# Requesting every second weight slab of the experts from ScalarE instead of SyncE

## The chip, the cores and the metric

The kernel runs on one core of a Trainium2 chip. The metric is the device time of one execution in microseconds (us). A core has five engines that run side by side, each with an instruction stream of its own: TensorE (PE), VectorE (DVE), ScalarE (ACT), GpSimd (POOL) and SyncE (SP), which here only issues DMA transfers. Transfers issued by SP run in the DMA queue that the profile calls q1, those issued by ACT in q10, and POOL's in q0. All the queues are served by the same 16 DMA engines.

## The reference

Two blocks of layers work on 256 tokens of width 1024. The first block has a short convolution, a SwiGLU layer, latent attention, and a mixture of eight experts. The second has four SwiGLU layers, block attention and a state-space mixer. The change touches the mixture alone:

```python
probs = jax.nn.softmax((ht @ router).astype(jnp.float32), axis=-1)
vals, idx = lax.top_k(probs, TOP_K)                      # TOP_K = 2
gates = ...                                              # the two weights of a token, zeros elsewhere
for e in range(N_EXPERTS):                               # 8
    out = out + gates[:, e:e + 1] * swiglu(ht, w_gate[e], w_up[e], w_down[e])   # hidden width 2048
```

## The kernel before

**Slabs.** All large weights are packed in the order of their use into 436 slabs of up to 128 x 2048 fp32 (1 MB). A slab is loaded from HBM into one of six slots of the SBUF tile `raw`. Then it is split in two, so that fp32 products can be built from fp32r products: ACT copies it, rounded, to `whi` (`split_hi`, L704 to L710), and DVE subtracts to get the rest, `wlo` (`split_lo`, L1298 to L1304). `whi` and `wlo` have three slots each. TensorE then makes three products per tile: high by high, high by low, low by high (`three`).

**Semaphores.** `raw_full[slot]` rises when a slab has landed. `slab_hi` counts ACT's copies, `slab_split` DVE's subtractions, and `slab_used` the slabs that TensorE is done with. ACT's copy of slab m waits until the slab has landed and until TensorE has used slab m - 3. The load of slab s waits for `slab_split >= s + 1`: the slab six places before has been split, so its slot is free.

**Queues.** SP issues all the slab loads, one after another, each as soon as its slot is free (`load`, L521 to L524). ACT issues few transfers, POOL a few small ones.

**The expert stage.** It has 8 experts with 24 slabs each, so 192 slabs, here called m = 0 to 191 (`ffn_stage` with `gates`). An expert's hidden width is cut in 8 chunks. Each chunk needs two slabs of gate and up weights and one of down weights. The program takes a step per slab: in step k of an expert, TensorE works on slab k, while ACT and DVE split slab k + 2 (`ahead`). No expert has more than 128 tokens to work on here, so the function `routed` runs: the tokens of an expert are gathered by small products with a 0/1 matrix (`gather` on TensorE, `operand` on ACT and DVE), and one tile of 128 rows goes through the layer. The function `ffn`, for more tokens, does not run in this stage.

**Results.** An expert's result, 128 x 1024, is copied from PSUM by ACT at step k = 2 of the next expert and stored to the DRAM tensor `y_rows`, from ACT's queue (`result`, L818 to L824). After the seventh such store has landed, POOL issues four indirect transfers that gather, for every token, the rows of its experts from `y_rows` back to SBUF (`y_back`, L617 to L623), 128 x 1024 each. DVE adds them to `x` in the last expert, at steps 13, 15, 18 and 20 (`add_back`, L1720 to L1725). The first of these waits until all four gathers have landed, and it stands in DVE's stream right behind the subtraction of slab m = 183. The subtraction of m = 184 comes behind it.

**What sets the order.** The streams of all engines are written out by hand; loops over the experts (`positions`, `each_expert`) repeat a body with register offsets. Nothing is scheduled by a planner.

Of the kernel before, what the change touches and what calls it, by code (L numbers as in the profile page):

```python
# [31 lines left out]
RAW = 6  # L32
SPLIT = 3
SLAB = 2048
EPS = 1e-6
F_EXPERT = 2048
D_FF = 2816
# [23 lines left out]
def program(nc, a, out):  # L61
    ctx = ExitStack()
    with ctx:
        def sb(name, shape, dt=F32):
            return ctx.enter_context(nc.sbuf_tensor(name, shape, dt))
# [4 lines left out]

        raw = sb("raw", [P, RAW, SLAB])
        whi = sb("whi", [P, SPLIT, SLAB], F32R)
        wlo = sb("wlo", [P, SPLIT, SLAB], F32R)
        raw_full = [sem(f"raw_full{n}") for n in range(RAW)]
        slab_hi = sem("slab_hi")
        slab_split = sem("slab_split")
# [442 lines left out]
        @block.sync  # L519
        def _(sp):  # L520
            def load(s, slot, width):  # L521

                sp.wait_ge(slab_split, s + 1)
                sp.dma_start(raw[:, slot, 0:width], slab_of(s, width)).then_inc(raw_full[slot], 16)  # L524

            def slab_of(s, width):
                return a["slabs"][s if isinstance(s, int) else bass.ds(s, 1)].rearrange(
                    "p n -> p n" if isinstance(s, int) else "o p n -> (o p) n")[:, 0:width]

            def ffn_loads(f):  # L530
                def at(k, i, ex):
                    load(f.s0 + k + 6 * i + 3 * f.C * ex, (f.s0 + k) % RAW, SLAB)
                positions(sp, f, at)

            for t in range(NT):
                sp.dma_start(x[:, t, :], a["x"].rearrange("(t p) d -> p t d", p=P)[:, t]).then_inc(x_loaded, 16)
            for f in stages_used:
                if f.kind == "ffn":
                    ffn_loads(f)
                else:  # L540
                    for n, width in enumerate(WIDTHS.get(f.kind, [])):
                        load(f.s0 + n, (f.s0 + n) % RAW, width)
            for n in range(2):
                cs = slice(512 * n, 512 * (n + 1))
                sp.wait_ge(x_ready, x_total - 1 + n)
                sp.dma_start(out.rearrange("(t p) d -> p t d", p=P)[:, :, cs], x[:, :, cs]).then_inc(out_done, 16)
            sp.wait_ge(out_done, 32)
# [155 lines left out]
        def _(act):  # L703
# [8 lines left out]
            def ahead(base, k, i=0, per=0):  # L712
                if base + k + 2 < total_slabs:
                    split_hi(base, k + 2, i, per)

            def squares(f):

                if f.x0 == 0:
                    act.wait_ge(x_loaded, 16 * NT)
                else:  # L720
                    act.wait_ge(x_ready, f.x0)
                for t in range(NT if f.deferred else 1):
                    act.activation(hn[:, t], x[:, t], ACT.Square, accum_out=n_sum[:, f.m, t:t + 1]).then_inc(norm_sum, 1)
# [34 lines left out]
            def ffn(f, opening=False, rest=False):  # L758
                C = f.C

                def t_hi(c, i, ex, to=hT):
                    act.wait_ge(tp_full, f.u0 + c + 1 + 2 * i + C * ex)
                    act.activation(to[0], tp[:, (f.u0 + c) % 2], ACT.Copy).then_inc(tp_hi, 1)  # L763

                def at(k, i, ex):
                    kind, c = ffn_kind(f, k, ex)
                    ahead(f.s0, k, i, C // 2 * ex)
                    if k == 0:
                        norm_late(f.before)
                        norm_squares(f.before)  # L770
                    if k == 1:
                        act.wait_ge(norm_rstd, f.m)
                    if kind == "up_b":
                        act.wait_ge(gu_half, f.c0 + c + 1 + 2 * i + C * ex)
                        act.activation(silu_g[:, 0, :], gu[:, 0, 0:FC], ACT.Silu,
                                       scale=n_rstd[:, f.m - 1, 0:1]).then_inc(gu_silu, 1)
                        used(act, f.s0, k, i, C // 2 * ex)
                        act.activation(silu_g[:, 1, :], gu[:, 1, 0:FC], ACT.Silu,  # L778
                                       scale=n_rstd[:, f.m - 1, 1:2]).then_inc(gu_silu, 1)
                    elif kind == "up_a" and k:  # L780
                        t_hi(c - 1, i, ex)
                    elif ends_with(f, k, ex):
                        t_hi(C - 1, 0, ex, hT_last)
                    elif kind == "down" and k == 3 * C - 1:
                        norm_early(f.after)
                positions(act, f, at, opening, rest)
# [13 lines left out]
            def routed(f):  # L800
                C = f.C
                v, g0 = V_FFN, KT

                def operand(q, kt, odd, base=2):

                    if kt % 4 == 0 and not odd:
                        act.wait_ge(gathered, 2 * q + kt // 4 + 1)
                    o = xg_odd if odd else xg_hi[0]
                    r = act.activation(o[:, kt * P:(kt + 1) * P], acc[in_pair(kt, odd, base)], ACT.Copy, scale=col(v, g0 + kt))
                    if kt % 2 and odd:  # L810
                        r.then_inc(xg_hi_done, 1)

                def odd_operand():

                    act.drain()
                    act.activation(xg_hi[1], xg_odd, ACT.Copy).then_inc(odd_hi_done, 1)

                def result(e, odd):  # L818

                    act.wait_ge(y_stored, 16 * e)  # L820
                    act.activation(y_out[odd], acc[:, 0:2, :].rearrange("p b n -> p (b n)"), ACT.Copy).then_inc(yg_hi_done, 1)
                    act.wait_ge(yg_hi_done, e)
                    act.dma_start(y_rows[(e - 1) * P:e * P] if isinstance(e, int) else y_rows[bass.ds((e - 1) * P, P)],
                                  y_out[odd]).then_inc(y_stored, 16)  # L824

                def last_result(n):

                    if n:
                        used(act, f.s0, 3 * C * EXPERTS - 1)
                    else:  # L830
                        act.wait_ge(y_half, 1)
                    act.activation(yg_hi[:, 512 * n:512 * n + 512], acc[:, n], ACT.Copy).then_inc(yg_hi_done, 1)

                def at(k, ex, first, last, pair):
                    kind, c = ffn_kind(f, k, ex)
                    if last and k == 3 * C - 1:
                        last_result(0)
                        last_result(1)
                    ahead(f.s0, k, 0, C // 2 * ex)
                    if k == 2 and not first:  # L840
                        used(act, f.s0, 1, 0, C // 2 * ex)
                        result(ex, 1 - pair[0])
                    if kind == "up_b":
                        used(act, f.s0, k, 0, C // 2 * ex)
                        act.activation(silu_g[:, 0, :], gu[:, c % 2, 0:FC], ACT.Silu).then_inc(gu_silu, 2)
                    t = 0 if first and k == 2 else c + 1 if kind == "down" and k != 3 * C - 1 else None
                    if t is not None:
                        act.wait_ge(tp_full, f.u0 + t + 1 + C * ex)
                        bank = tp[:, (f.u0 + t) % 2]
                        if t == 1 and last:  # L850
                            act.activation(put, bank[:, 2 * P:4 * P], ACT.Copy)
                        to = hT_spare if last and t == C - 1 else hT
                        act.activation(to[0][:, 0:2 * P], bank[:, 0:2 * P], ACT.Copy).then_inc(tp_hi, 1)
                    odd, q = pair
                    if odd and not last:
                        for n in range(2):
                            if GATHER_AT[n] < k <= GATHER_AT[n] + 4:
                                for j in range(2):
                                    operand(q + 1, 4 * n + k - GATHER_AT[n] - 1, j)
                    if not odd and k == ODD_AT:  # L860
                        odd_operand()

                act.sem_inc(y_stored, 16)
                for kt in range(KT):
                    for j in range(2):
                        operand(0, kt, j, (2, 0)[kt // 4])
                each_expert(act, at)

            def mla(f):
# [2235 lines left out]
```

## Time and profile before

| | |
|---|---|
| device time, median of 3 runs | 2086.67 us (2085.4 to 2086.81) |
| span of the profiled execution | 2084.0 us |
| busy: PE, DVE, ACT, POOL | 98%, 68%, 57%, 5% |
| TensorE clock granted | 1.000 throughout |
| moved by DMA | 467.11 MB, of it 455.24 MB in q1 |
| expert stage, about 425 to 978 us of the span | 339 to 384 GB/s in slices of 52 us; elsewhere 305 at the start, then 122 to 195 GB/s |

The span runs from the first to the last instruction of one profiled execution; it is the only time that the profile gives for it. The 2.7 us between it and the median lie around the span. All times of the trace below count from the start of the span. "Landing" is the time from the start of a DMA issue to the semaphore that tells of its end. An engine's name with a q (ACTq, SPq) marks an instruction of its sequencer, the part that waits and issues, while the engine's own arithmetic may go on. A row names the line of the code, so L1303 is the subtraction that makes `wlo`, L710 the copy that makes `whi`.

### The profile page before, as it was taken

The numbers are of one execution on the slowest core, as the hardware profiler recorded it, in microseconds if no ns is written. First come the engines' busy times: TensorE is split into PE (matmuls) and PEld (weight loads), VectorE is DVE, ScalarE is ACT, GpSimd is POOL, SyncE is SP. The second block draws the span as 40 slices with busy tenths as digits, with TensorE's granted clock in tenths as the row PEclk, the third lists the DMA queues.
The fourth block names the chain that finished last, engine by engine and source line by source line (L and its number), as shares of the span: only waits on it lengthen the run. The fifth ranks groups of instructions, "written<-read, shape, count | busy, mean of one in ns | idle before, by whom it ended". The sixth has DMA issues, their size and how long they took to land.

```text
span 2084.0 us, 27770 instructions
## 1 busy us (share of the span) xinstructions
PE 2046.0 (98%) x10189; PEld 1713.0 (82%) x10189; DVE 1409.6 (68%) x1529; ACT 1198.0 (57%) x1374; POOL 93.9 (5%) x140
## 2 busy tenths in 40 slices
PE   9999999999999999999999999999999999999999
PEld 9988887778878878787788877888888899888887
DVE  6655457698888988889444685445555579785444
ACT  4454458677777777776344565444444465874442
POOL 1010001000000000010100010000000000220000
PEclk9999999999999999999999999999999999999999
DMA  8555434389999999998555443555455455445551
GB/s 305 187 183 185 180 140 145 122 326 362 361 362 370 357 362 351 367 384 339 183 185 194 160 164 145 185 195 184 178 184 181 147 180 194 162 152 182 190 192 41
DMA packets 68267, 467.11 MB, mean 224 GB/s; under 512 B 7776, under 2 KB 8176, under 8 KB 13520
## 3 DMA queue, kind: packets, MB, share of 16 engines
q1 hardware_dynamic: 63616, 455.24, 59.0%
q10 hardware_dynamic: 3536, 8.10, 1.2%
q0 software_dynamic: 1024, 2.56, 0.5%
q8 instruction: 57, 0.93, 0.2%
q14 instruction: 34, 0.28, 0.0%
HBM read 461.11 MB, written 4.75 MB: 224 GB/s over the span
## 4 chain that ended last, share of the span: by engine, by line
PE 84%; DVE 6%; ACT 5%; issue 3%; DVEq 1%; ACTq 0%; POOL 0%; POOLq 0%
PE gu L2146 15%; PE gu L2148 15%; PE gu L2147 15%; PE acc L2146 9%; PE acc L2148 9%; PE acc L2147 9%; DVE wlo L1303 3%; ACT whi L710 2%; PE acc L2242 2%; PE acc L2244 2%; PE acc L2243 2%; PE tp L2256 1%; PE tp L2175 1%; PE acc L2696 1%; PE tp L2728 1%
## 5 line engine op out<-in xcount | busy, mean ns | idle before, releaser
L1303 DVE TENSOR_TENSOR wlo<-raw,whi 128x2048 fp32r<-128x2048 f32 (+2 forms) x435 | 987.1, 2272 | 365.6 <-ACT whi L710 365.2
L710 ACT ACTIVATE whi<-raw 128x2048 fp32r<-128x2048 f32 (+1 forms) x436 | 827.4, 1899 | 214.5 <-PE acc L2148 165.9
L2146 PE MATMUL gu<-whi,actA_hi 128*128 128x512 f32 (+1 forms) x1448 | 575.4, 397 | 3.6 <-DVE actA_lo L1324 1.5
L2147 PE MATMUL gu<-wlo,actA_hi 128*128 128x512 f32 (+1 forms) x1448 | 563.0, 389 | 1.3 <-issue 1.3
L2148 PE MATMUL gu<-whi,actA_lo 128*128 128x512 f32 (+1 forms) x1448 | 564.0, 389 | 0.0
L2146 PEld LDWEIGHTS gu<-whi,actA_hi 128*128 128x128 f32 x1448 | 272.0, 188 | 59.8 <-issue 5.3
L2148 PEld LDWEIGHTS gu<-whi,actA_lo 128*128 128x128 f32 x1448 | 271.7, 188 | 59.1 <-issue 1.5
L2147 PEld LDWEIGHTS gu<-wlo,actA_hi 128*128 128x128 f32 x1448 | 272.4, 188 | 52.0
L2146 PE MATMUL acc<-whi,hT_hi 128*128 128x512 f32 x656 | 256.6, 391 | 4.4 <-DVE wlo L1303 4.1
L2148 PE MATMUL acc<-whi,hT_lo 128*128 128x512 f32 x656 | 255.6, 390 | 0.0
L2147 PE MATMUL acc<-wlo,hT_hi 128*128 128x512 f32 x656 | 255.4, 389 | 0.0
L2146 PEld LDWEIGHTS acc<-whi,hT_hi 128*128 128x128 f32 x656 | 123.1, 188 | 33.4 <-DVE wlo L1303 3.8
L763 ACT ACTIVATE hT_hi<-tp 128x512 fp32r<-128x512 f32 x50 | 29.9, 598 | 202.2 <-PE tp L2256 202.2
L2148 PEld LDWEIGHTS acc<-whi,hT_lo 128*128 128x128 f32 x656 | 123.2, 188 | 25.8
L2147 PEld LDWEIGHTS acc<-wlo,hT_hi 128*128 128x128 f32 x656 | 123.2, 188 | 24.8
L1371 DVE TENSOR_TENSOR hT_lo<-tp,hT_hi 128x512 fp32r<-128x512 f32 x50 | 34.6, 692 | 117.6 <-ACT hT_hi L763 117.6
L2146 PE MATMUL acc<-whi,actA_hi 128*128 128x512 f32 (+1 forms) x240 | 98.0, 409 | 0.0
L778 ACT ACTIVATE silu_g<-gu,n_rstd 128x256 f32<-128x256 f32 x55 | 26.1, 475 | 119.3 <-PE gu L2148 119.3
L2148 PE MATMUL acc<-whi,actA_lo 128*128 128x512 f32 (+1 forms) x240 | 91.7, 382 | 0.0
L2147 PE MATMUL acc<-wlo,actA_hi 128*128 128x512 f32 (+1 forms) x240 | 91.4, 381 | 0.0
L1386 DVE SCALAR_TENSOR_TENSOR h_tok<-gu,n_rstd,silu_g 128x256 f32<-128x256 f32 x110 | 52.9, 481 | 48.0 <-ACT silu_g L778 47.9
L2242 PE MATMUL acc<-actB_hi,whi 128*128 128x256 f32 x256 | 73.2, 286 | 0.5 <-DVE wlo L1303 0.5
(448 smaller groups left out, 2257.2 us busy)
## 6 DMA issues: line engine op xcount, KB each, us to landing
raw<-in_slabs SPq DMA_DIRECT2D x427, 1024.0 KB, 4.9
y_rows<-big ACTq DMA_DIRECT2D x7, 512.0 KB, 7.4
raw<-in_slabs SPq DMA_DIRECT2D x4, 576.0 KB, 3.7
hT_hi<-cum_rows ACTq DMA_DIRECT2D x8, 256.0 KB, 3.1
hT_lo<-cum_rows ACTq DMA_DIRECT2D x8, 256.0 KB, 4.3
raw<-in_slabs SPq DMA_DIRECT2D x2, 768.0 KB, 4.1
raw<-in_slabs SPq DMA_DIRECT2D x2, 640.0 KB, 3.9
x<-in_x SPq DMA_DIRECT2D x2, 512.0 KB, 4.8
```

The costliest lines, as they stand in the source:

```text
L710: act.activation(whi[:, n0 % SPLIT, 0:w], raw[:, n0 % RAW, 0:w], ACT.Copy).then_inc(slab_hi, 1)
L763: act.activation(to[0], tp[:, (f.u0 + c) % 2], ACT.Copy).then_inc(tp_hi, 1)
L778: act.activation(silu_g[:, 1, :], gu[:, 1, 0:FC], ACT.Silu, scale=n_rstd[:, f.m - 1, 1:2]).then_inc(gu_silu, 1)
L1303: dve.tensor_tensor(wlo[:, n0 % SPLIT, 0:w], raw[:, n0 % RAW, 0:w], whi[:, n0 % SPLIT, 0:w].bitcast(F32), ALU.subtract).then_inc(slab_spli ...
L1371: dve.tensor_tensor(to[1], tp[:, (f.u0 + c) % 2], to[0].bitcast(F32), ALU.subtract).then_inc(tp_read, 1)
L1386: dve.scalar_tensor_tensor(h_tok[:, t, :], gu[:, t, FC:2 * FC], n_rstd[:, f.m - 1, t:t + 1], silu_g[:, t, :], ALU.mult, ALU.mult).then_inc ...
L2146: pe.matmul(o, xh, wh, start=start, stop=False)
L2147: pe.matmul(o, xh, wl, start=False, stop=False)
L2148: return pe.matmul(o, xl, wh, start=False, stop=stop)
L2242: pe.matmul(o, w[0][:, kt, bs], aT_hi[:, kt], start=kt == 0, stop=False)
L2243: pe.matmul(o, w[0][:, kt, bs], aT_lo[:, kt], start=False, stop=False)
L2244: r = pe.matmul(o, w[1][:, kt, bs], aT_hi[:, kt], start=False, stop=kt == KT - 1)
```

## The change

SP asks only for some of the slabs of the expert stage: the first nine (m = 0 to 8) and after them those with even m. The odd ones, m = 9, 11, ..., 191, are asked for by ACT in its own queue: at step k (odd), behind the copy of slab k + 2, ACT waits for the same semaphore value and issues the load of slab k + 6. These are 92 loads. Slots, semaphores, splitting and products stay as they are, and so do the loads of all other stages.

```diff
+BESIDE = 6
+FIRST_BESIDE = 3 + BESIDE
...
+            def expert_loads(f):
+                n = 3 * f.C
+                def at(k, ex, first):
+                    if k % 2 == 0 or (first and k < FIRST_BESIDE):
+                        load(f.s0 + k + n * ex, (f.s0 + k) % RAW, SLAB)
+                for k in range(n + 2):
+                    at(k, 0, True)
+                with sp.Fori(1, f.experts - 1) as ex:
+                    for k in range(2, n + 2):
+                        at(k, ex, False)
+                for k in range(2, n):
+                    at(k, f.experts - 1, False)
...
-                if f.kind == "ffn":
+                if f.kind == "ffn" and f.gates is not None:
+                    expert_loads(f)
+                elif f.kind == "ffn":
                     ffn_loads(f)
...
+            def load_beside(f, k, ex):
+                n = 3 * f.C
+                m = k + BESIDE
+                if f.gates is None or m % 2 == 0 or isinstance(ex, int) and n * ex + m >= n * f.experts:
+                    return
+                s = f.s0 + m + n * ex
+                act.wait_ge(slab_split, s + 1)
+                act.dma_start(raw[:, (f.s0 + m) % RAW, :], a["slabs"][s if isinstance(s, int) else bass.ds(s, 1)].rearrange(
+                    "p n -> p n" if isinstance(s, int) else "o p n -> (o p) n")).then_inc(raw_full[(f.s0 + m) % RAW], 16)
...
                     ahead(f.s0, k, 0, C // 2 * ex)
+                    load_beside(f, k, ex)
                     if k == 2 and not first:
                         used(act, f.s0, 1, 0, C // 2 * ex)
                         result(ex, 1 - pair[0])
```

Where ACT's stream changes: the start of an expert in the loop, where the result of the expert before it is stored (`y_rows<-big`). Before, from the store on, with the copies of two slabs:

```order
305 L821 ACTIVATE big<-acc 128x1024 [waits y_stored]
306 L823 ISA [waits yg_hi_done]
307 L823 DMA y_rows<-big 128x1024
308 L708 REGISTER_ALU [waits raw_full2]
309 L710 ACTIVATE whi<-raw 128x2048 [waits slab_used]
310 L449 REGISTER_ALU
311 L845 ACTIVATE silu_g<-gu 128x256 [waits slab_used]
312 L710 ACTIVATE whi<-raw 128x2048 [waits slab_used,raw_full3]
```

The same place of ACT's stream now (the lines have moved: L710 is L729, L823 is L855; the load is L743):

```order
317 L853 ACTIVATE big<-acc 128x1024 [waits y_stored]
318 L855 ISA [waits yg_hi_done]
319 L855 DMA y_rows<-big 128x1024
320 L727 REGISTER_ALU [waits raw_full2]
321 L729 ACTIVATE whi<-raw 128x2048 [waits slab_used]
322 L742 ISA
323 L743 ISA [waits slab_split]
324 L743 DMA raw<-in_slabs 128x2048
325 L451 REGISTER_ALU
326 L878 ACTIVATE silu_g<-gu 128x256 [waits slab_used]
327 L729 ACTIVATE whi<-raw 128x2048 [waits slab_used,raw_full3]
```

A load with its wait and a register instruction now stands between the copy of 128x2048 and the silu behind it. It is in the same queue as the store just ahead of it.

Where SP's stream changes: the end of its loop over the experts and the loads of the last expert behind it. Before (L524 is the load, L461 the loop over the experts, L472 that of the next stage):

```order
102 L523 REGISTER_ALU
103 L524 ISA [waits slab_split]
104 L524 DMA raw<-in_slabs 128x2048
105 L461 REGISTER_ALU
106 L461 COMPARE_AND_BRANCH
107 L524 DMA raw<-in_slabs 128x2048 [waits slab_split] x24
108 L472 UNCONDITIONAL_BRANCH
```

The same place of SP's stream now:

```order
66 L525 REGISTER_ALU
67 L526 ISA [waits slab_split]
68 L526 DMA raw<-in_slabs 128x2048
69 L546 REGISTER_ALU
70 L546 COMPARE_AND_BRANCH
71 L526 DMA raw<-in_slabs 128x2048 [waits slab_split] x13
72 L474 UNCONDITIONAL_BRANCH
```

The 24 loads in a row of before are 22 of the last expert and the first two of the next stage. Of these 13 are left with SP; of the other 11 slabs the loads are ACT's. The streams of PE, DVE and POOL are the same as before.

## Rows read from the trace of the kernel before

**Rows 1.** Windows: length, PE busy, PEld, DVE, ACT, POOL, clock, DMA share, GB/s.

```profile
431.00:925.00 494.00, 487.40 (x2220) 396.62 (x2219) 430.94 (x321) 372.51 (x338) 0.45 (x1) 1.00 0.95 363
925.00:956.00 31.00, 29.93 (x135) 24.05 (x134) 28.76 (x20) 22.11 (x19) 7.64 (x4) 1.00 1.00 411
```

**Rows 2.** Waits of PE in the expert stage, 430 to 970: total, times, longest.

```profile
PE tp L2728 <- DVE h_tok L1739: 4.4, 8, 0.9
PE acc L2146 <- DVE wlo L1303: 3.0, 5, 0.7
```

**Rows 3.** The slab loads, line L524, 431 to 925.

```profile
L524 SPq DMA_DIRECT2D raw<-in_slabs x168: 327/333/343, 431.6 to 924.6; - x168
DMA to landing us min/median/max: 4.7/6.8/9.3
```

**Rows 4.** The first and the last of the four gathers, line L621, with their landings.

```profile
L621 POOL DMA_INDIRECT big<-y_rows,back_row x1: 1187/1187/1187, 924.5 to 924.5; - x1
DMA to landing us min/median/max: 10.0/10.0/10.0
...
L621 POOL DMA_INDIRECT big<-y_rows,back_row x1: 2577/2577/2577, 931.0 to 931.0; - x1
DMA to landing us min/median/max: 14.8/14.8/14.8
```

**Rows 5.** DMA queues, 929 to 943: packets, MB, share of 16 engines.

```profile
q1 hardware_dynamic: 521, 3.82, 65.7%
q0 software_dynamic: 539, 1.97, 35.4%
```

**Rows 6.** Timeline of DVE at the first `add_back` (L1724): start, length.

```profile
944.35 2.29 DVE L1303 TENSOR_TENSOR wlo<-raw,whi 128x2048 fp32r<-128x2048 f32 x1 [0.37 <-ACT whi L710]
946.73 1.29 DVE L1724 SCALAR_TENSOR_TENSOR x<-big,x 128x1024 f32<-128x1024 f32 x1
...
948.27 4.48 DVE L1303 TENSOR_TENSOR wlo<-raw,whi 128x2048 fp32r<-128x2048 f32 x2
```

**Rows 7.** Timeline of PE where slab m = 184 begins.

```profile
950.61 0.50 PE L2146 MATMUL acc<-whi,hT_hi 128*128 128x512 f32 x1 [0.17 <-DVE wlo L1303]
```

**Rows 8.** The seven stores of results, line L823; below, the landing of the last alone.

```profile
L823 ACTq DMA_DIRECT2D y_rows<-big x7: 343/347/374, 487.8 to 914.0; - x7
DMA to landing us min/median/max: 4.6/7.4/10.4
...
DMA to landing us min/median/max: 9.6/9.6/9.6
```

**Rows 9.** Timeline of ACT in the state-space stage: a DMA issue without a wait.

```profile
1785.37 0.63 ACT L1142 ACTIVATE aux<-aux 128x512 f32<-128x512 f32 x1
1785.37 0.33 ACTq L1125 DMA_DIRECT2D hT_hi<-cum_rows  x1
1785.90 1.90 ACT L710 ACTIVATE whi<-raw 128x2048 fp32r<-128x2048 f32 x1
```

**Rows 10.** Timeline of ACT behind the last store, which had waited for its copy.

```profile
914.42 1.92 ACT L710 ACTIVATE whi<-raw 128x2048 fp32r<-128x2048 f32 x1 [0.49 <-ACT big L821]
```

**Rows 11.** Waits of ACT in the expert stage, 430 to 970.

```profile
ACT silu_g L845 <- PE gu L2148: 52.7, 54, 3.2
ACT hT_hi L853 <- PE tp L2728: 50.8, 56, 2.7
ACT whi L710 <- PE gu L2148: 25.1, 45, 0.7
```

**Rows 12.** The load of slab m = 185, line L524, with its landing.

```profile
L524 SPq DMA_DIRECT2D raw<-in_slabs x1: 328/328/328, 935.3 to 935.3; - x1
DMA to landing us min/median/max: 11.3/11.3/11.3
```

**Rows 13.** Timeline of ACT: the copies of slabs m = 181 and m = 185.

```profile
936.87 1.91 ACT L710 ACTIVATE whi<-raw 128x2048 fp32r<-128x2048 f32 x1
...
947.81 1.92 ACT L710 ACTIVATE whi<-raw 128x2048 fp32r<-128x2048 f32 x1 [0.62 <-PE gu L2148]
```

More of the change, by code:

```diff
@@ L767, in at @@
                     ahead(f.s0, k, i, C // 2 * ex)
+                    if k >= 2:
+                        load_beside(f, k, ex)
                     if k == 0:
@@ L839, in at @@
                     ahead(f.s0, k, 0, C // 2 * ex)
+                    load_beside(f, k, ex)
                     if k == 2 and not first:
```

## The prediction, made before the changed kernel ran

> **What bounds the kernel now.** I read the busy shares by window first. In the expert stage TensorE is busy 487.40 of 494 us and the clock is granted in full; DVE (430.94) and ACT (372.51) have time left [rows 1]. The DMA engines are busy 95% at 363 GB/s, and 100% at 411 GB/s in the last 31 us [rows 1], so the second question is whether a slab is ever late. The waits say no. TensorE waits 7.4 us in the whole stage, and both rows name DVE [rows 2]. ACT's waits, which would hold a late slab, all name TensorE [rows 11]. A load takes 4.7 to 9.3 us to land until 925 [rows 3]. So the loads have time, though little bandwidth is free. I then looked for the other users of the DMA engines in the stage, because the change touches nothing but queues: ACT's seven stores of results [rows 8] and POOL's four gathers [rows 4], which use the queue q0 beside q1 [rows 5]. Last came what waits for them: DVE's first `add_back` [rows 6], and behind it TensorE [rows 7].
>
> **Part 1: 92 issues come to ACT.** An issue takes about 0.35 us of ACT's sequencer [rows 8]. In the state-space stage such an issue starts in the same instant as an ACTIVATE of 0.63 us, and the next ACTIVATE starts 0.53 us later, at the usual 0.1 us before the end of the one ahead [rows 9]. So an issue that waits for nothing runs beside the arithmetic and costs nothing. Here each new issue stands behind a copy of 1.9 us [rows 13] and waits for `slab_split` at a value that belongs to slab m - 6, which TensorE is about to use or using; in nearly all steps it is there. The other end is the store, which has to wait for its copy: ACT then idles 0.49 us in front of the next copy [rows 10]. At that price 92 issues are 45 us of ACT, but ACT waits 128.6 us in the stage (52.7 + 50.8 + 25.1) [rows 11], 0.67 us a step. Only where it does not wait would the price show: the 7 turns from expert to expert and the 12 odd steps (9, 11, 17 and 19 of experts 1, 3 and 5) in which it also makes the next operands. That is 19 x 0.49 = 9.3 us at most. I take 0, since rows 9 is the same kind of instruction in the same position; the cover is the copy.
>
> **Part 2: the odd slabs are asked for later.** SP asked for slab m as soon as its slot was free; ACT asks when its copy of slab m - 4 has begun. For m = 185 that is 936.87 instead of 935.3, 1.6 us later [rows 12, 13]. SP's request came 12.5 us before the copy of the slab at 947.81 [rows 12, 13]; 10.9 us would be left, and until 925 the slowest landing is 9.3 us [rows 3]. Cost 0 there. At m = 185 the landing took 11.3 us, because the gathers run at that time, and the copy would be 0.4 us late if it stayed so [rows 12, 13]; that is the upper end, and it lies inside the delay of part 4.
>
> **Part 3: SP loses 92 issues.** SP waited for free slots before each, and nothing waits for SP. 0.
>
> **Part 4: a third queue beside the gathers.** This is the term that I find. From 929 to 943 the queues q1 (slabs) and q0 (gathers) both have work all the time. They are served packet for packet, 521 against 539, which gives 3.82 against 1.97 MB in 14 us, 414 GB/s together [rows 5]. The first gather lands at 924.5 + 10.0 = 934.5, the fourth at 931.0 + 14.8 = 945.8 [rows 4]: three intervals of 3.77 us. A gather is 128 x 1024 fp32, 0.524 MB, so 1.27 us of each interval are its own at 414 GB/s and 2.50 us are q1's. Now the slabs come in two queues. If each queue takes its turn, a gather needs 1.27 + 2 x 2.50 = 6.27 us. The fourth then lands three such intervals behind the first, at 934.5 + 18.8 = 953.3. That holds while both slab queues have work. Together they would get 5.00 of 6.27 us of 414 GB/s, 330 GB/s, and the stage wants 363 [rows 1], so their backlog grows and they stay full.
>
> What waits for it: DVE has done the subtraction of m = 183 at 944.35 + 2.29 = 946.64 and starts the first `add_back` at 946.73 [rows 6]. The fourth gather had landed 0.9 us before. Landing at 953.3, it holds DVE for 6.6 us. Behind the `add_back` stand DVE's part of the hidden rows and the subtraction of m = 184 [rows 6]. TensorE already waits 0.17 us for just this subtraction [rows 7], so there is no slack, and the 6.6 us go to the end in full; ACT and SP, which follow TensorE and DVE by semaphores, shift along. The later three `add_back` find their data in place.
>
> The bounds. Upward: the first gather is stretched too, by one more slab's share, 2.5 us, so 9.1 us. Downward: the gathers start when the last store has landed, which took 9.6 us, with other stores at 4.6 [rows 8]. Beside half the slabs in q1 it could land up to 5.0 us sooner, so 1.6 us. The slabs themselves gain from the third turn in this stretch, but ACT does not wait for them [rows 11], so 0. I take 6.6, because the gathers' own spacing is the nearest row.
>
> The Trainium skill (page "DMA: Bandwidth & Descriptors", section "Queues, rings and completion order") says that each DMA engine goes round robin between the queue rows that it has work for, packet by packet. No row here shows three full queues at once; by that rule the third turn is real and the second rival below falls. The rule's packet may hold several descriptors, where the trace's records of q1 and q0 alternate one for one; for the spacing both give the same.
>
> **Sum.** 2084.0 (span) + 0 + 0 + 0 + 6.6 = 2090.6 us; with the 2.7 us that lie around the span before (2086.67 - 2084.0) this is 2093.3 us. I forecast 2093.
>
> **Rivals.**
> First, ACT pays for its issues: they do not hide under the copy. For it: the 0.49 us of rows 10. Against it: rows 9, and ACT's waits. Price 9.3 us: 2096.
>
> Second, on the other side, no change: the gathers keep every second turn, because the DMA engines take the two slab queues in one turn, or one of them is always empty when the other is full. Then the fourth gather lands before 946.7, DVE waits for nothing, and everything else hides under TensorE. For it: all rows show but two queues at a time, and at 363 of 411 GB/s [rows 1] a slab queue may run dry for a while. It decides as soon as the fourth gather is less than 0.9 us later than before. Time: 2086.7. In between, if a store that lands sooner gives most of the delay back, the time is 2088 to 2090.
>
> Third, faster: two queues feed the DMA engines more evenly, slabs land sooner, and some of the 7.4 us of TensorE's waits [rows 2] go. Against it: both rows name DVE, which itself waits for no slab. At most 2086.7 - 7.4 = 2079, more likely 2082.
>
> **How the numbers follow.** The third queue that holds up the gathers: 0.60, at 2093, its own range 2088 to 2096. No change: 0.27, at 2086.7. ACT pays: 0.08, at 2096. Faster: 0.05. What a measurement of this kernel can tell from no change is 0.2%, 4.2 us, so 2082.5 to 2090.9 is "same". Of the first case about 0.10 falls below 2090.9. Slower: 0.50 + 0.08 = 0.58; same: 0.27 + 0.10, less a little at the edge, 0.37; faster: 0.05. The range from 2085.5 to 2097 holds the no-change case, the forecast and its upper end, and leaves out the faster case and a little above.
>
> **What would show it.** In the profile after: q10 with some 96 MB more and q1 with as much less. The gathers of L621 about 6.3 us apart in their landing instead of 3.8, the last at 953 or so. In DVE's rows a wait of 6 to 7 us in front of the first `add_back`, put down to POOL's DMA, and one of the same length of TensorE for `wlo` behind it. ACT's waits for TensorE otherwise about as before, ACT's DMA issues starting within 0.5 us of the start of a copy, and no wait of ACT for a slab. The expert stage up to 925 as long as before, to 1 us. Part 4 is wrong if the gathers keep their spacing, or if the last store lands so early that they are done by 946.7. Part 1 is wrong if ACT's copies start later behind TensorE than before. The forecast as a whole is wrong if the stretch from 925 to 978 is no longer than now.

## The result, and the profile after

| | before | changed |
|---|---|---|
| median of 9 runs | 2085.87 us (2085.34 to 2087.02) | 2091.1 us (2089.43 to 2093.45) |
| ratio to before, 95% interval | | 1.0026, 1.0017 to 1.0035 |
| span of the profiled execution | 2084.0 us | 2091.7 us |

The change costs 5.2 us. The forecast was 2093.3 us, a loss of 6.6 us, all of it from a third full DMA queue beside the gathers. The profiled execution of the changed kernel is the slowest of its nine (2093.45 us), so what the profile shows is more than the 5.2 us of the medians. The line numbers have moved: L524 is L526, L710 is L729, L1303 is L1336, L1724 is L1757, L621 is L640, L823 is L855. ACT's loads of slabs are L743.

First, is the loss spread over the stage? Up to 925 us it is not. The window of 494 us before the gathers, with columns as in [rows 1]:

```profile
431.00:925.00 494.00, 487.72 (x2222) 396.85 (x2221) 431.22 (x321) 372.44 (x338) 4.63 (x2) 1.00 0.95 362
```

TensorE is as busy as before (487.72 against 487.40 us), at full clock. The copies of the slabs start within 0.7 us of their times before, up to m = 183. ACT's own issues hide. Two of them on ACT's timeline:

```profile
572.15 1.91 ACT L729 ACTIVATE whi<-raw 128x2048 fp32r<-128x2048 f32 x1
572.25 0.34 ACTq L743 DMA_DIRECT2D raw<-in_slabs  x1
```

The issue begins 0.1 us after the copy and is over long before it. ACT waits for TensorE as much as before, 50.8, 55.4 and 24.3 us where [rows 11] has 52.7, 50.8 and 25.1; the 4.6 us more in the second are the stall below.

What the two queues do change, all along the stage, is how long a slab takes to land. The slab loads of ACT and then of SP, up to 925, where [rows 3] has a median of 6.8 and a maximum of 9.3:

```profile
DMA to landing us min/median/max: 4.7/7.9/10.7
...
DMA to landing us min/median/max: 4.8/8.0/10.3
```

TensorE never waits for it there, but the margin is thin. From the landing of a slab to its copy there were at least 3.7 us before (m = 8 to 175); now it is 0.2 us at m = 81. Not all of the longer landing need be the change's: two other kernels with SP alone (e3b, e7) have a median of 5.6 to 5.7 us there, where this profile of before has 6.8. Behind 925 us the margin is gone. Slab m = 185 landed 11.6 us after its request, and its copy had to wait:

```profile
948.40 1.92 ACT L729 ACTIVATE whi<-raw 128x2048 fp32r<-128x2048 f32 x1 [1.11 <-DMA raw<-in_slabs]
```

The copy began 0.6 us later than before [rows 13]. It cost nothing here, because DVE, which needs it next, was held up for longer by the gathers.

Now the gathers. The first and the last of the four, as in [rows 4]:

```profile
L640 POOL DMA_INDIRECT big<-y_rows,back_row x1: 2297/2297/2297, 920.1 to 920.1; - x1
DMA to landing us min/median/max: 11.8/11.8/11.8
...
L640 POOL DMA_INDIRECT big<-y_rows,back_row x1: 2687/2687/2687, 928.1 to 928.1; - x1
DMA to landing us min/median/max: 23.1/23.1/23.1
```

They land at 931.9 and 951.2: three intervals of 6.4 us, where before there were 3.77. And they start 4.4 us sooner, since the last store, which took 9.6 us [rows 8], now takes this:

```profile
DMA to landing us min/median/max: 5.1/5.1/5.1
```

The last store lands sooner in every kernel in which ACT asks for slabs at that place (3.0 to 5.7 us) than in those in which SP asks for all the slabs there (7.7 to 9.6 us).

The queues from 929 to 943, where [rows 5] has two, with packets, MB and share:

```profile
q10 hardware_dynamic: 332, 2.45, 41.7%
q1 hardware_dynamic: 304, 2.20, 37.9%
q0 software_dynamic: 340, 1.26, 22.1%
```

The three queues get 332, 304 and 340 packets: equal turns. The gathers' 1.97 MB of before have become 1.26 MB. DVE at the first `add_back`, where [rows 6] shows no wait:

```profile
951.30 1.28 DVE L1757 SCALAR_TENSOR_TENSOR x<-big,x 128x1024 f32<-128x1024 f32 x1 [4.57 <-DMA big<-y_rows,back_row]
```

And TensorE at slab m = 184, where [rows 7] has a wait of 0.17 us:

```profile
955.17 0.79 PE L2179 MATMUL acc<-whi,hT_hi 128*128 128x512 f32 x1 [4.64 <-DVE wlo L1336]
955.76 0.63 PE L2180 MATMUL acc<-wlo,hT_hi 128*128 128x512 f32 x1
```

The reader should look at the lengths too: 0.63 us for a product that takes 0.39 elsewhere. The windows show why, in the column behind POOL, the granted clock:

```profile
956.00:960.00 4.00, 4.00 (x10) 3.07 (x10) 3.91 (x4) 0.00 (x0) 0.00 (x0) 0.50 0.77 256
...
987.00:992.00 5.00, 4.29 (x12) 3.43 (x13) 3.54 (x5) 2.18 (x3) 0.00 (x0) 0.66 0.16 25
```

TensorE stands still from 950.5. The granted clock falls to 0.50 at 953.8, still within the wait, and is back at 960.6; 0.50 is the lower of its two levels (1.2 instead of 2.4 GHz). It falls once more from 987.9 to 991.3, where the stage ends and TensorE has waited 1.5 us as it does before (1.49 us there too); in the profile of before, the clock stayed at 1.00 there.

By the starts of the copies against those of before, the shift is 0.1 us at m = 183, 6.0 us at m = 187, and 7.7 us from four slabs into the next stage to the end. So of the 7.7 us of this execution, 4.6 are the wait, 1.4 the low clock behind it, and 1.7 the second fall of the clock. This second fall is not peculiar to the changed kernel. The profile of e6 below, a kernel without any stall of DVE or TensorE at the gathers, has the same fall at the same place, and the copies slip by 1.6 us there:

```profile
979.00:984.00 5.00, 4.36 (x12) 3.44 (x13) 3.47 (x5) 2.12 (x2) 0.00 (x0) 0.66 0.10 15
```

The nine runs fall into two groups: in five the mean clock is 0.999, with 2089.4 to 2091.1 us, in four 0.997, with 2091.5 to 2093.5. A stretch of 6.8 us at half clock takes 0.0016 off the mean and the low clock at the end of the span up to 0.0003 more, so a run with only the first fall of the profile would show 0.998, as e11 does. In the five runs, the median one among them, the clock was thus low for a shorter time. Where, no profile shows; runs of the kernel before have a mean of 0.999 too, from 2085.4 us up.

### The profile page after: what moved, and what is told of

It reads as the page before. It is cut to its first block, busy times and chain, and to the rows that moved or that the text cites. A ratio compares the mean times of both kernels' runs of the same rounds, so it can differ in the third digit from the quotient of the medians.

```text
span 2091.7 us, 27698 instructions
## 1 busy us (share of the span) xinstructions
PE 2049.5 (98%) x10189; PEld 1715.4 (82%) x10189; DVE 1409.3 (67%) x1529; ACT 1197.5 (57%) x1374; POOL 95.5 (5%) x140
## 4 chain that ended last, share of the span: by engine, by line
PE 82%; DVE 6%; ACT 5%; issue 3%; DMA 2%; DVEq 1%; ACTq 1%; POOL 0%; SPq 0%; POOLq 0%
PE gu L2179 15%; PE gu L2181 15%; PE gu L2180 15%; PE acc L2179 9%; PE acc L2181 9%; PE acc L2180 9%; DVE wlo L1336 3%; ACT whi L729 2%; PE acc L2275 2%; PE acc L2277 2%; PE acc L2276 2%; PE tp L2289 1%; DMA big<-y_rows,back_row 1%; PE tp L2208 1%; PE acc L2729 1%
## 5 line engine op out<-in xcount | busy, mean ns | idle before, releaser
L1336 DVE TENSOR_TENSOR wlo<-raw,whi 128x2048 fp32r<-128x2048 f32 (+2 forms) x435 | 986.9, 2271 | 367.9 <-ACT whi L729 367.3
L729 ACT ACTIVATE whi<-raw 128x2048 fp32r<-128x2048 f32 (+1 forms) x436 | 827.3, 1899 | 216.0 <-PE acc L2181 161.9
```

Source lines behind the costliest of these rows:

```text
L729: act.activation(whi[:, n0 % SPLIT, 0:w], raw[:, n0 % RAW, 0:w], ACT.Copy).then_inc(slab_hi, 1)
L1336: dve.tensor_tensor(wlo[:, n0 % SPLIT, 0:w], raw[:, n0 % RAW, 0:w], whi[:, n0 % SPLIT, 0:w].bitcast(F32), ALU.subtract).then_inc(slab_spli ...
```

## The experiments

The theory is that of the prediction: the third full queue beside the four gathers. The rivals: ACT pays for its issues, and slabs come late all along the stage. Each time below is a median, beside runs of the kernel before on the same chip (2085.6 to 2085.9 us). The intervals of the ratios reach about 0.0009, or 1.9 us, to either side, so smaller differences are not told apart from nothing. Where the text prices a smaller one, it goes by the traces.

**e1: the last expert's loads by SP alone.**

```diff
-                if f.gates is None or m % 2 == 0 or isinstance(ex, int) and n * ex + m >= n * f.experts:
+                if f.gates is None or m % 2 == 0 or isinstance(ex, int) and ex == f.experts - 1:
```

SP's loads of the last expert take every k from 9 on.

> The changed kernel, but in the last expert SP asks for the odd slabs too (m = 177 to 191), so ACT issues 84 loads instead of 92, and none while the gathers run. Theory (a third busy queue beside the four gathers delays the first add_back): the gathers land 3.8 us apart again, DVE does not wait for them, and the time is that of before, 2086 us, within 1.5 us. Rival (ACT pays for each issue): 84 of 92 issues are left, so 84/92 of the 5.2 us stay, 2090.6 us. Rival (two queues make slabs late throughout the stage): also about 2090.5 us.

Measured: 2085.54 us, ratio 0.9999 (0.9990 to 1.0008). The first and the last gather:

```profile
L641 POOL DMA_INDIRECT big<-y_rows,back_row x1: 2405/2405/2405, 922.9 to 922.9; - x1
DMA to landing us min/median/max: 10.0/10.0/10.0
...
L641 POOL DMA_INDIRECT big<-y_rows,back_row x1: 2579/2579/2579, 930.7 to 930.7; - x1
DMA to landing us min/median/max: 13.5/13.5/13.5
```

They land at 932.9 and 944.3, 3.8 us apart, and DVE does not wait. The 84 loads that ACT still issues cost nothing that these runs can tell. Slabs land just in time here too: the copies wait 1.8 us for them, four times in all, at no visible cost. So both rivals fall as the cause of the 5.2 us, and without eight loads of the last expert there is no loss. Whether these eight alone make the whole of it is asked next.

**e2 and e10: only the last expert's odd slabs by ACT.** The other half, run twice.

```diff
-                    if k % 2 == 0 or (first and k < FIRST_BESIDE):
+                    if k % 2 == 0 or not (isinstance(ex, int) and ex == f.experts - 1) or k < FIRST_BESIDE:
...
-                if f.gates is None or m % 2 == 0 or isinstance(ex, int) and n * ex + m >= n * f.experts:
+                if f.gates is None or m % 2 == 0 or not (isinstance(ex, int) and ex == f.experts - 1) or m >= n:
```

> The other half: SP asks for all slabs of the experts 0 to 7, except for the odd ones m = 177 to 191, which ACT asks for. Only 8 issues come to ACT. Theory: the whole loss is here; the last gather lands at 950 to 953, DVE waits 4 to 7 us, time 2090 to 2092 us. Rival (ACT pays per issue): 8/92 of 5.2 us, 2086.4 us. Rival (late slabs all along the stage): at most 1 us of loss, 2087 us.

> e2_last_expert_by_act once more, for a second profile. Its 11 times lay between 2085.3 and 2093.7 us; in its profile the last store took 3.0 us to land and the last gather landed at 947.3, 0.7 us too late. Theory: the time follows the landing of the last gather. A profile in which it lands at T shows DVE's wait T - 946.7, and the time is about 2086 us plus this wait, plus 1 to 3 us where TensorE's clock falls.

Measured: 2087.26 us, ratio 1.0009 (1.0000 to 1.0018), with single runs from 2085.3 to 2093.7; the second run (e10, a single time) took 2087.96 us. This was not the 2090 to 2092 us that I expected: the eight loads are needed for the loss (e1), but alone they make only some 1.4 us. The mechanism is there: the gathers land 6.1 and 6.3 us apart. But the store took 3.0 us, so they began at 917.8, and the last one landed at 947.3 in the first profile and 948.7 in the second. DVE's wait in the first:

```profile
DVE x L1757 <- DMA big<-y_rows,back_row: 0.9, 1, 0.9
```

The second run does not fit the rule written for it: DVE was late itself by then and waited 0.2 us only, while the copies of slabs had slipped by up to 2.4 us one after another from m = 179 on, because slabs landed late: ACT waited 5.5 us for them in four waits, for m = 179, 181, 183 and 185, all its own. The price came in another way, 2.0 us in the end. So late slabs, the rival that e1 put aside, can cost time too, though only in this stretch. What differs from the changed kernel is what lies in the queues when the gathers begin. In e2 a slab took 5.6 us (median) to land up to then, in the changed kernel 8, and there the store (5.1 us) and the first gather (11.8 against 11.0) are slower too. That the 3.8 us between e2 and the changed kernel come from this backlog fits the traces, but it was not isolated.

**e5: all slabs of the last expert by ACT, from m = 176 on.** The condition `m % 2 == 0` goes, and SP's loads of the last expert end at k = 7.

> SP asks for all slabs up to m = 175, ACT for all 16 from m = 176 on. While the gathers run there are again only two full queues, q10 (slabs) and q0, and ACT issues twice as many loads there as in the changed kernel. Theory (number of full queues): the gathers land 3.8 us apart, DVE waits at most 1 us, 2086 to 2087 us. Rival (what counts is that ACT issues loads in this stretch): worse than with the odd ones alone, 2092 us or more.

Measured: 2086.45 us, ratio 1.0003 (0.9994 to 1.0012). The gathers land at 927.1 and 938.8, 3.9 us apart, and DVE does not wait. Twice the loads from ACT in the very stretch, but two full queues instead of three: for the spacing of the gathers the number of queues decides, not who issues.

**e3 and e3b: the adds later.** In the changed kernel and, as control, in the one before.

```diff
-BACK_AT = (13, 15, 18, 20)
+BACK_AT = (16, 18, 20, 22)
```

> The changed kernel with the four add_back at steps 16, 18, 20 and 22 of the last expert instead of 13, 15, 18 and 20. The first then stands where DVE arrives at about 955, behind the last landing at 951. Theory: the gathers still land 6.3 us or more apart, but nobody waits for them; time 2086 to 2088 us, where the 2 us above before are for the adds that now stand closer to the end of the stage. TensorE's clock stays at its full share, since there is no stall. Rival (ACT pays, or the slabs are late): the loss stays, 2091 us.

> The kernel before with the four add_back at steps 16, 18, 20 and 22. Control for e3_late_add_back (2087.3 us): if the 1.4 us that e3 keeps are the price of the late adds, this one takes 2087.3 us too; if they come from the third queue, 2085.9 us.

Measured: e3 2087.31 us, ratio 1.0007 (0.9998 to 1.0016); e3b 2086.03 us, ratio 1.0001 (0.9993 to 1.0010). In e3 the last gather lands at 951.5, as late as in the changed kernel, and the first `add_back` finds it there:

```profile
955.56 1.28 DVE L1757 SCALAR_TENSOR_TENSOR x<-big,x 128x1024 f32<-128x1024 f32 x1
```

The clock of the profiled execution stays at 1.000. So some 3.8 of the 5.2 us are the wait with its clock, taken away with the queues as they are. The late adds cost nothing that e3b can tell. Of the 1.4 us that e3 keeps, its interval holds nothing as well; if they are real, they are not the price of the late adds, as I had written, but may be late slabs. In its trace the copies wait 2.3 us, four times, for slabs that have not landed (`ACT whi L729 <- DMA raw<-in_slabs: 2.3, 4, 1.7`).

**e7: the stall alone.** The kernel before, with `BACK_AT = (11, 15, 18, 20)`.

> The kernel before with the first add_back at step 11 instead of 13. DVE gets there at 941.1 and the last gather lands at 945.8, so it makes DVE wait 4.7 us with no change of the queues. It prices the stall alone. If a stall costs its length, 2085.9 + 4.5 = 2090.4 us. If TensorE's clock falls behind it, as it did in the changed kernel (0.50 from 956 to 960), 1.5 to 3 us more: 2092 to 2093 us.

Measured: 2086.19 us, ratio 1.0011 (1.0001 to 1.0021), and the median says little: eight of the twelve runs lie between 2085.4 and 2088.3 us, four between 2091.1 and 2096.3, these at a mean clock of 0.997 or 0.998. The profiled one is among the eight:

```profile
943.99 1.28 DVE L1724 SCALAR_TENSOR_TENSOR x<-big,x 128x1024 f32<-128x1024 f32 x1 [3.08 <-DMA big<-y_rows,back_row]
```

A wait of 3.1 us gave a span 2.5 us longer, with the clock at 1.00. I had reckoned with a wait of 4.7 us, but here the last store landed sooner. Seven of the eight runs took at most 2086.3 us, no more than before; how long DVE waited in them is not known, so this kernel prices no stall of 4.6 us. It does show that a stall can pass without the clock's falling. Which stall does so is open, and its length alone does not tell: TensorE's wait was 3.3 us here, and in e4 below a wait of 2.4 us was followed by a fall.

**e4 and e6: all slabs by ACT, in its loop and with the loop written out.** In e4 ACT issues 184 loads; in e6 its loop over the experts is unrolled besides.

```diff
-                    if k % 2 == 0 or (first and k < FIRST_BESIDE):
+                    if first and k < FIRST_BESIDE - 1:
...
-                if f.gates is None or m % 2 == 0 or isinstance(ex, int) and n * ex + m >= n * f.experts:
+                if f.gates is None or isinstance(ex, int) and n * ex + m >= n * f.experts:
...
-                each_expert(act, at)          # e6 only
+                for e in range(EXPERTS):
+                    for k in range(2, 3 * (F_EXPERT // FC) + (0 if e == EXPERTS - 1 else 2)):
+                        at(k, e, e == 0, e == EXPERTS - 1, (e % 2, e // 2))
```

> ACT asks for all slabs of the experts from m = 8 on (184 loads), SP for none of them. Twice the issues on ACT, but again one slab queue beside the gathers. Theory: the gathers land 3.8 us apart again and the loss is gone, 2086 us, unless the last store, which now stands behind slabs in its own queue, lands later than the 9.6 us of before: each us of that is a us of wait from 0.9 us on, 2086 to 2089 us. Rival (ACT pays per issue): twice the 5.2 us, 2096 us.

> As e4_all_by_act (ACT asks for all slabs from m = 8 on), but ACT's loop over the experts is written out, with constants in place of registers. e4 lost its 9.6 us in two jumps, 3.2 us and 5.1 us, at the first step of the second and the third pass of ACT's loop, not in equal parts per issue. If the jump back is what costs (the longer loop body has to be brought in again), the loss is gone: 2086 to 2087 us. If it is the issues, it stays: 2095 us.

Measured: e4 2095.5 us, ratio 1.0046 (1.0032 to 1.0059); e6 2084.22 us, ratio 0.9992 (0.9983 to 1.0000). Taken alone e4's time is what the rival "ACT pays per issue" gave. Its trace says otherwise. The gathers are 3.8 us apart, and the time goes in two places, m = 76 and m = 124. These are the first steps of the second and the third pass of ACT's loop:

```profile
630.30 1.92 ACT L729 ACTIVATE whi<-raw 128x2048 fp32r<-128x2048 f32 x1 [2.98 <-PE gu L2181]
...
778.23 1.91 ACT L729 ACTIVATE whi<-raw 128x2048 fp32r<-128x2048 f32 x1 [4.74 <-issue]
```

The slabs had landed 9 us before, so ACT waited for none of them. Nor was it TensorE, which the profile names at the first place: it ran without a gap until 632, 0.3 us behind its times of before, and there the same copy began at 627.2. TensorE waited 2.4 and 4.2 us for the `wlo` behind these copies. After each wait the clock was at 0.50 for 3.4 us, which makes up much of what is left of the 9.6 us over before: the shift is 2.8 us at m = 76 and 0.6 more by m = 80. From there to the second place, some 45 steps with an issue each, it grows by 0.6 us. With the loop written out, both stops are gone, and 184 issues from ACT cost nothing (e6 against e8 below, 2084.22 and 2084.18 us). That the jump brings in the loop body again and finds it late is my reading; shown is only that the stops go with the loop.

**e8, e9 and e11: the written-out loop by itself.** e8 is the kernel before with ACT's loop unrolled as in e6, e9 has DVE's unrolled too, and e11 is the changed kernel with ACT's unrolled.

> The kernel before (SP asks for all slabs) with ACT's loop over the experts written out. e6_all_by_act_unrolled took 2084.2 us, 1.7 less than before. If that gain is the written-out loop (constants in place of register instructions, no jump back), it is here too: 2084.2 us. If it comes from ACT's asking for the slabs, this one takes 2085.9 us.

> As e8_before_act_unrolled, and DVE's loop written out too. DVE is the engine that TensorE waits for in this stage (7.4 us in all). If register instructions delay DVE as they delay ACT, up to 1 us less than e8; else the same as e8.

> The changed kernel with ACT's loop written out. Theory (third full queue beside the gathers): the loss of 5.2 us does not depend on the loop, so it stays on top of e8's time: 2089.5 us, the gathers 6.2 to 6.5 us apart. Rival (the changed kernel loses by its longer loop body on ACT, as e4 did): no loss against e8, 2084.2 us.

Measured: e8 2084.18 us, ratio 0.9993 (0.9984 to 1.0002); e9 2084.05 us, 0.9992 (0.9983 to 1.0001); e11 2089.56 us, 1.0017 (1.0008 to 1.0026). So the loss of the change, 5.4 us between e11 and e8, does not depend on the loop. e11's profile is the cleaner one of the two, with one fall of the clock only, from 950.6 to 957.5. Its copies slip by 5.5 us at the stall, 4.6 of them DVE's wait, as long as in the changed kernel:

```profile
DVE x L1759 <- DMA big<-y_rows,back_row: 4.6, 1, 4.6
```

e8, e9 and e6 are the fastest kernels here, by some 1.5 us over before. Each interval alone touches 1, but the three agree, and in e8's trace the copies draw ahead of those of before step by step, mostly at the turns of the experts, to 1.8 us in all. At six of the seven turns ACT idles 0.46 to 0.48 us behind the store, in place of 0.64 to 0.92. That this is the cause of the gain was not isolated.

## Why the prediction was right

**Part 1, ACT's issues at 0: right.** 75 of the 92 start within 0.3 us of the start of a copy and end under it; the other 17 start up to 0.9 us away, at no cost that the trace shows. e1 (84 issues), e5 (16 in the critical stretch) and e6 (184) show it by their times.

**Part 2, odd slabs later, 0 up to 925: right for the time, wrong in what I looked at.** I took the landing times of before over unchanged. The median went from 6.8 to 8, for SP's loads as well. Up to 925 nothing waited, but the margin that I put at 10.9 against 9.3 us came down to 0.2 us at one slab. At m = 185 the copy was 0.6 us late, where I had 0.4 as the upper end, and ACT did wait for a slab (1.1 us), which I had written would not happen. It lay inside the delay of part 4, as said there. In e10 such lateness was the price itself.

**Part 3, SP: right**, nothing waits for it.

**Part 4, the third queue: right in mechanism and place, and off in three sizes that partly cancel.** The interval of the gathers was put at 6.27 us and is 6.4. The last landing was put at 953.3 and is 951.2, since the store landed 4.5 us sooner. I had named this as the lower bound (up to 5.0 us) and gave it no weight; against it, the first gather was stretched, which I had as the upper bound (2.5 us; it took 11.8 instead of 10.0 us). So DVE's wait was 4.6 us and not 6.6. What no term of the sum had is the clock. "The 6.6 us go to the end in full" counts a stall at its length, but TensorE worked at half clock behind it: 5.5 us for a wait of 4.6 in e11, 6.0 in the profiled execution of the changed kernel. The further 1.7 us of that execution are the second fall of the clock, which is not the change's (e6). By how much the stall was lengthened in the other eight runs is not known; a mean clock below 1.000, which all nine have, does not show it, since runs of the kernel before have one too.

**The sum.** 2093.3 was 2.2 us too high. Of these, 1.4 are the loss (6.6 against 5.2) and 0.8 the base: the median before was 2086.67 us of three runs and is 2085.87 of nine. The 2.7 us that I added as lying around the span were too much as well. In every run with both figures, time and span differ by 1.7 to 1.8 us. That the loss came out so near is in part luck: the sooner store took 4.4 us off the landing, the first gather and the spacing put 2.3 back, and the clock added what nobody had counted.

The round robin between queue rows, which the Trainium skill (page "DMA: Bandwidth & Descriptors", section "Queues, rings and completion order") states and no row before the change could show for three queues, agrees with the trace after: 332, 304 and 340 packets.

The rival "no change" had 0.27. Its mechanism, gathers that keep every second turn, fell with their spacing of 6.4 us; its time would have been right for a kernel with the adds three steps later (e3, 2087.3 us). The rival "ACT pays" fell with e1, e5 and e6. The rival "faster" fell too: slabs landed later, not sooner.

## What to carry to other kernels

A second issuing queue for the same stream was not neutral here, with the DMA engines 95% busy: each full queue got an equal turn (332, 304 and 340 packets), so a third party's transfers lost share, and whoever waited for them paid. Before moving transfers to another queue, list every other transfer in that stretch and the slack of its waiter; here it was 0.9 us. If a wait appears, move the consumer (e3) or keep the stream in one queue while the other transfers run (e1, e5). And read the granted clock behind every new stall of TensorE, in more than one profile: the fall at the end of the stage is there in the changed kernel and in e6, and not in e3 and e11.

## What the runs showed that was not expected

- A stall of TensorE of 4.6 us brought 6.8 us at clock 0.50, the last 5.4 of them with TensorE at work, and products of 0.63 instead of 0.39 us. Waits of 2.4 and 4.2 us in e4 brought 3.4 us each. The wait of 3.3 us in e7's profile brought none.
- The seven stores of results land in 5.1 us (median) in the changed kernel, where the profile of before has 7.4, though they share their queue with slabs. Only part of that is the change: with SP alone, e3b and e7 have medians of 5.4 and 5.5.
- ACT's loop over the experts with a load in each step (e4) stopped for 3.0 and 4.7 us at its two jumps back, and both stops are gone with the loop (e6). With half the loads in the body (the changed kernel) no such stop is seen.
